# Order of the recurrence and seven waits' places in a three-product float32 decoder kernel, with GpSimd's hold one piece later

## The chip, the cores and the metric

The kernel runs on one core of a Trainium2 chip. Six processors work side by side on it: TensorE (matmuls, results in eight PSUM banks of 128 x 512 float32), VectorE, ScalarE (which loads a table before a new family of functions), GpSimd, SyncE, which issues transfers, and the DMA engines. Each runs its own list of instructions in order and waits for others by semaphores. The metric is the time of one execution in microseconds (us), as a median over runs.

## The reference, cut to what matters

Two blocks over 512 tokens of width 1024, batch 1. The first block has two layers: layer 0 mixes by a bidirectional gated linear recurrence (HGRN2, 8 heads of 128), layer 1 by latent attention (16 heads). Each layer then has an MLP and a gated embedding ("ple"):

```
for i in range(DEPTH):                       # 2 layers
    a = rms_norm(h, pre_mix_norm[i])
    m = hgrn2_mixer(a, ...) if i == 0 else mla_mixer(a, ...)
    h = h + rms_norm(m, post_mix_norm[i])
    f = squared_relu_mlp(rms_norm(h, pre_mlp_norm[i]), w_mlp_in[i], w_mlp_out[i])
    h = h + rms_norm(f, post_mlp_norm[i])
    e = p[i] @ w_ple_proj[i]
    g = sigmoid(h @ w_ple_gate[i])
    h = h + rms_norm(g * e, ple_norm[i])

def step(state, inp):                        # one chunk of the recurrence
    q_dec, k_inv, k_end = qi * exp(G), ki * exp(-G), ki * exp(G_last - G)
    attn = where(mask, q_dec @ k_inv.T, 0)
    o = attn @ vi + q_dec @ state
    new_state = exp(G_last) * state + k_end.T @ vi
```

The recurrence runs forward and backward, and its two outputs are added, normed and multiplied by silu(gate). The second block (names ending in _2) has a differential attention of four heads beside a convolution of 31 taps, a cross attention to a memory of 256 rows (w_ckv_2 gives its keys and values), and a convolutional feed-forward net. Everything is float32.

## The kernel before

**Tiles.** Activations lie feature-major: eight tiles of 128 features x 512 tokens. A float32 matmul is made of three faster ones: each operand x is split into a high half xH, rounded to a shorter type, and a low half xL = x - xH, and TensorE adds H·H, H·L and L·H (`three`, the lines L479 to L481; where three column blocks of weights run side by side, L577 to L582). Weights come from HBM in pieces of 128 rows x 512, in the order of a list PLAN that `plan()` writes. GpSimd splits piece after piece in `split_piece`: a tensor_scalar makes wH (L2775), a tensor_tensor wL (L2777). There are seven split buffers, so piece n waits until TensorE is done with piece n - 7. ScalarE makes the high halves of activations (aH, uH) and VectorE the low halves (aL, uL).

**Hold.** `behind[n] = "x0"` in `plan()` makes GpSimd wait, before it splits piece n, until VectorE has made the last low half of the stream x0 (`add_normed`: the residual plus a normed value, then the norm for the next matmuls). There are six such holds: x (into the MLP), hs (into the gate of the embedding) and n (into the next layer), for each of the two layers. In each, the weights of three column blocks are opened first (`open3`), so that TensorE can take each tile of the stream as it comes.

**Recurrence.** For each head, `recur` in `pe` does for one direction after the other three things: it transposes k_end (L634, "keT"; ScalarE copies the result to g_kT, "kT"), makes the scores (L641, "S"; VectorE masks them), and the states (L650, "U", which read g_kT and the values g_Vt; VectorE accumulates them, "St"). `outputs` (L659) then multiplies the masked scores, summed over both directions in g_As, with the values. Between them stand projections for the next head, and for the last head (7) steps of the out projection. ScalarE in its head loop does the sigmoids of the next head's forget gates and this head's gate ("sg", `sigmoid_g`), then `recur` (the copies kT), then logarithms and decays; for head 7 only the gate's sigmoid, `exp_table()` and `recur`. VectorE does in the same order the gate's product (`out_gate`) and `recur`.

**Norms.** A norm's sum of squares over the features is made by VectorE adding squares of tiles 0 to 6 ("sum") and by two matmuls with ones in `stat_end` (L512 for the sum, L515 for the squares of the last tile, "sq"); ScalarE takes the root as exp(-0.5 ln), for which it needs another table than for the sigmoid. For "ple" ScalarE squares tiles 0 to 6 and VectorE tile 7, after its last sum; ScalarE loads the table for exp and ln meanwhile.

**Around them.** At the start TensorE does the projections of head 0 in the order forward gate, backward gate, statistics "a1", q, out gate, values. In layer 1, between the gate and the next stream, stand the keys of the memory (`memory_keys(0)` ahead of the statistics "ple", `memory_keys(2)` behind). In the differential attention, `d_normed(hd)` on VectorE makes a head's normed output and at once its low half uL, for which it waits for ScalarE's uH; `d_turned(hd + 1)` rescales the next head's attention.

## Time and profile before

| | |
|---|---|
| median of 3 runs | 2334.65 us (2334.12 to 2335.09) |
| profiled execution: its time / its span | 2332.7 us / 2330.9 us |
| TensorE busy | 98% of the span |
| VectorE, ScalarE, GpSimd busy | 55%, 28%, 67% |
| mean granted clock of TensorE | 0.995 |
| chain of work that ended last | TensorE 91%, VectorE 5%, GpSimd 3%, ScalarE 1% |

A row of the trace's order of time begins with the start in us from the start of the span and the duration; then come engine, line, operation, output<-inputs by the program's names, shapes, and the number of instructions that were joined in the row. In brackets stands how long the engine sat idle before it, and what ended the idle time. The granted clock is the share of full speed, 2.4 GHz; 0.5 would be 1.2 GHz.

### The profile page before, as it was taken

What the parts mean: (1) busy time and instruction counts of PE and PEld (TensorE: products, weight loads), DVE (VectorE), ACT (ScalarE), POOL (GpSimd) and SP (SyncE); (2) the same over time, 40 slices, a digit from 0 to 9 for tenths busy, and PEclk for the clock granted to TensorE, in tenths of its full rate; (3) what the DMA queues carried; (4) which work ended last, traced back from release to release, by engine and by line L of the source; (5) the groups of instructions that cost most, each with busy time, mean ns of one, the idle gap of its engine ahead of it and who ended that gap; (6) DMA issues with size and microseconds to landing.
All of it is one profiled execution on the core that took longest, in us unless ns stands there. A gap on an engine that the chain in (4) does not pass through costs nothing.

```text
span 2330.9 us, 27596 instructions
## 1 busy us (share of the span) xinstructions
PE 2280.3 (98%) x10430; PEld 1855.1 (80%) x10430; DVE 1282.2 (55%) x1825; ACT 653.0 (28%) x1202; POOL 1568.7 (67%) x1532
## 2 busy tenths in 40 slices
PE   8999999999999899999999999999999999999998
PEld 6888877888887688888778888787668788888887
DVE  7774737245245777175544364469865445626354
ACT  3443433101013455154311010132344232202113
POOL 8556557877776654644497777678426947878784
PEclk9999999999999999999999999999999999999999
DMA  5222222333332211211243333333212422333332
GB/s 170 77 73 82 72 82 77 109 99 95 100 95 77 72 38 32 81 41 54 69 121 106 96 110 103 95 87 109 64 37 77 122 56 94 99 96 96 99 95 77
DMA packets 112725, 200.16 MB, mean 86 GB/s; under 512 B 12496, under 2 KB 21200, under 8 KB 112592
## 3 DMA queue, kind: packets, MB, share of 16 engines
q1 hardware_dynamic: 109424, 194.72, 29.0%
q10 hardware_dynamic: 3168, 3.67, 0.5%
q8 instruction: 83, 1.36, 0.2%
q14 instruction: 50, 0.41, 0.1%
HBM read 196.24 MB, written 2.10 MB: 85 GB/s over the span
## 4 chain that ended last, share of the span: by engine, by line
PE 91%; DVE 5%; POOL 3%; ACT 1%; issue 0%; DMA 0%; SPq 0%; DVEq 0%; POOLq 0%
PE bank L479 26%; PE bank L481 26%; PE bank L480 26%; POOL wL L2777 2%; PE bank L916 1%; DVE bank L1936 1%; DVE h L1928 1%; POOL wH L2775 1%; PE bank L1040 1%; DVE aL L1936 1%; PE bank L512 1%; PE bank L885 1%; PE bank L887 1%; PE bank L886 1%; PE bank L893 1%; PE bank L894 1%
## 5 line engine op out<-in xcount | busy, mean ns | idle before, releaser
L2777 POOL TENSOR_TENSOR wL<-raw,wH 128x512 fp32r<-128x512 f32 (+2 forms) x732 | 1002.9, 1370 | 61.1
L2775 POOL TENSOR_SCALAR wH<-raw 128x512 fp32r<-128x512 f32 (+2 forms) x732 | 530.0, 724 | 587.3 <-PE bank L481 496.8
L479 PE MATMUL bank<-aH,wH 128*128 128x512 f32 x1376 | 546.5, 397 | 12.7 <-DVE aL L1936 7.0
L481 PE MATMUL bank<-aH,wL 128*128 128x512 f32 x1376 | 536.6, 390 | 0.0
L480 PE MATMUL bank<-aL,wH 128*128 128x512 f32 x1376 | 536.5, 390 | 0.0
L479 PE MATMUL bank<-uH,wH 128*128 128x512 f32 (+1 forms) x978 | 378.4, 387 | 0.0
L481 PE MATMUL bank<-uH,wL 128*128 128x512 f32 (+1 forms) x978 | 376.8, 385 | 0.0
L480 PE MATMUL bank<-uL,wH 128*128 128x512 f32 (+1 forms) x978 | 376.8, 385 | 0.0
L479 PEld LDWEIGHTS bank<-aH,wH 128*128 128x128 f32 x1376 | 258.4, 188 | 73.3 <-POOL wL L2777 13.8
L480 PEld LDWEIGHTS bank<-aL,wH 128*128 128x128 f32 x1376 | 258.6, 188 | 56.5 <-issue 4.1
L481 PEld LDWEIGHTS bank<-aH,wL 128*128 128x128 f32 x1376 | 258.4, 188 | 54.7
L480 PEld LDWEIGHTS bank<-uL,wH 128*128 128x128 f32 x978 | 183.7, 188 | 37.4 <-issue 0.7
L479 PEld LDWEIGHTS bank<-uH,wH 128*128 128x128 f32 x978 | 183.7, 188 | 37.4 <-issue 0.7
L481 PEld LDWEIGHTS bank<-uH,wL 128*128 128x128 f32 x978 | 183.7, 188 | 36.7
L1299 ACT ACTIVATE uH<-mr 128x512 fp32r<-128x512 f32 x64 | 40.5, 633 | 391.0 <-DVE mr L1936 391.0
L1928 DVE TENSOR_TENSOR F<-F,bank 128x512 f32<-128x512 f32 x56 | 38.4, 686 | 190.1 <-PE bank L481 190.1
L1936 DVE SCALAR_TENSOR_TENSOR mr<-bank,rs 128x512 f32<-128x512 f32 x64 | 44.0, 688 | 156.6 <-PE bank L481 140.7
L1936 DVE SCALAR_TENSOR_TENSOR bank<-F,vs,bank 128x512 f32<-128x512 f32 x138 | 103.7, 751 | 35.7 <-ACT bank L1299 22.7
L1928 DVE TENSOR_TENSOR sums<-sums,sq 128x512 f32<-128x512 f32 (+1 forms) x66 | 81.8, 1240 | 69.9 <-ACT sq L1299 69.7
L1928 DVE TENSOR_TENSOR h<-h,bank 128x512 f32<-128x512 f32 (+1 forms) x91 | 60.7, 668 | 97.6 <-PE bank L481 95.9
L2784 POOL TENSOR_SCALAR m_P<-m_P,m_stat 128x512 f32<-128x512 f32 x64 | 44.6, 698 | 92.5 <-DVE m_stat L2370 90.4
L1936 DVE SCALAR_TENSOR_TENSOR c_cb<-c_xb,vs,c_cb 128x511 f32<-128x511 f32 x88 | 82.8, 941 | 40.3 <-ACT c_cb L1299 38.7
(328 smaller groups left out, 3208.9 us busy)
## 6 DMA issues: line engine op xcount, KB each, us to landing
raw<-in_ws SPq DMA_DIRECT2D x698, 256.0 KB, 2.6
raw<-in_ws SPq DMA_DIRECT2D x24, 192.0 KB, 2.3
h<-in_xT SPq DMA_DIRECT2D x8, 256.0 KB, 5.5
E<-in_memT ACTq DMA_DIRECT2D x16, 128.0 KB, 2.7
raw<-in_ws SPq DMA_DIRECT2D x10, 128.0 KB, 2.2
tmp<-in_pT ACTq DMA_DIRECT2D x4, 256.0 KB, 3.2
out<-c_F SPq DMA_DIRECT2D x2, 512.0 KB, 2.9
out<-c_F SPq DMA_DIRECT2D x2, 384.0 KB, 2.9
```

Of the source, the lines that this page charges most:

```text
L479: P.e.matmul(o, lH, rH, start=start, stop=False, skip_group_check=skip)
L480: P.e.matmul(o, lH, rL, start=False, stop=False, skip_group_check=skip)
L481: return P.e.matmul(o, lL, rH, start=False, stop=stop, skip_group_check=skip)
L512: i = P.e.matmul(b.ap[:, 0:n], ones, sums[:, 0:n], start=True, stop=not tail)
L885: P.e.matmul(b.ap[:, :], m_qnH[:, c], m_knH[:, :], start=True, stop=False)
L886: P.e.matmul(b.ap[:, :], m_qnH[:, c], m_knL[:, :], start=False, stop=False)
L1299: return A.e.activation(o, i, func, bias=bias, scale=scale)
L1928: return V.e.tensor_tensor(o, a, b, op)
L1936: return V.e.scalar_tensor_tensor(o, a, s, b, op0, op1)
L2775: G.e.tensor_scalar(H, x, 1.0, 0.0, MUL, ADD).then_inc(*G.did("wH", n))
L2777: G.e.tensor_tensor(L, x, H.bitcast(F32), SUB).then_inc(*G.did("w", n))
L2784: G.e.tensor_scalar(x, x, m_st[:, 4 * (hd % 2) + n, 2:3], 0.0, MUL, ADD).then_inc(*G.did("mP", hd, n))
```

## The change

Seven things are moved, all in the order of work; what is computed stays, only the place where a square is made changes.

1. `plan()`: each hold stands one piece later in the list, so GpSimd splits one piece more before it waits for VectorE (three places in `mlp_ple`, which is called for two layers: six holds).
2. `stat_end` and the embedding: ScalarE squares all eight tiles of "ple", and VectorE's square of tile 7 goes; ScalarE loads its table after the eighth square.
3. `pe`, `recur`: both directions' transposes, then both directions' scores, then both directions' states.
4. Start: the projection of q stands ahead of the statistics "a1".
5. Layer 1: both steps of the memory's keys stand behind the statistics "ple".
6. ScalarE and VectorE, head loop: for heads 0 to 6 the order is as before; for head 7 `recur` stands ahead of the gate's sigmoid, its product and the table load.
7. VectorE, differential attention: the low half of `d_normed` is a function of its own, `d_normed_low`, and stands behind the turning of the next head.

```diff
--- before.py
+++ after.py
@@ -79,21 +79,21 @@
     def mlp_ple(layer, *keys_next):
         embed(layer, 0)
         open3(*[("w_mlp_in", layer, 128 * o) for o in range(3)])
-        behind[len(out)] = f"x{layer}"
+        behind[len(out) + 1] = f"x{layer}"
         for g in range(4):
             for i in range(0 if g else 3, 8):
                 tile8("w_mlp_in", layer, 1024 * g + 128 * i)
             down("w_mlp_out", layer, tuple(range(8 * g, 8 * g + 8)), g == 0)
         embed(layer, 1)
         open3(*[("w_ple_gate", layer, 128 * o) for o in range(3)])
-        behind[len(out)] = f"hs{layer}"
+        behind[len(out) + 1] = f"hs{layer}"
         for o in range(3, 8):
             tile8("w_ple_gate", layer, 128 * o)
         if layer:
             for o in range(4):
                 tile8("w_ckv_2", 0, 128 * o)
         open3(*keys_next)
-        behind[len(out)] = f"n{layer}"
+        behind[len(out) + 1] = f"n{layer}"
 
     mlp_ple(0, *[("mla_w_in", 0, 128 * o) for o in (3, 4, 0)])
     for i in (1, 2):
@@ -511,7 +511,7 @@
                 P.wait_ge(cs_in)
                 i = P.e.matmul(b.ap[:, 0:n], ones, sums[:, 0:n], start=True, stop=not tail)
                 if tail:
-                    P.wait_ge(V if sid[0] == "ple" else A, "sq", sid, tiles - 1)
+                    P.wait_ge(A, "sq", sid, tiles - 1)
                     i = P.e.matmul(b.ap[:, 0:n], ones, sq[:, 0:n], start=False, stop=True)
                 i.then_inc(*P.did("stat", *sid))
                 if adds:
@@ -634,6 +634,7 @@
                         i = P.e.transpose(b.ap[:, cols128(n)], g_ke[d][:, cols128(n)], ident)
                     i.then_inc(*P.did("keT", head, d))
                     give(b, A, "kT", head, d)
+                for d in range(2):
                     b = take("S", head, d)
                     P.wait_ge(V, "ki", head, d)
                     P.wait_ge(V, "qd", head, d)
@@ -642,6 +643,7 @@
                                        start=True, stop=True)
                     i.then_inc(*P.did("S", head, d))
                     give(b, V, "Ab", head, d)
+                for d in range(2):
                     b = take("U", head, d)
                     P.wait_ge(A, "kT", head, d)
                     P.wait_ge(A, "Vt", head // 4, 3)
@@ -676,9 +678,9 @@
 
             project(0, 1)
             project(0, 2)
+            project(0, 0)
             stat_end("a1")
-            for part in (0, 3):
-                project(0, part)
+            project(0, 3)
             project_v(0)
             columns("a1")
             for head in range(8):
@@ -792,12 +794,11 @@
                 for o in range(3, 8):
                     linear(("gate", i, o), (A, "sg", i, o), "w_ple_gate", i, 128 * o, aH, aL, hs_ready)
                 P.also("gate done", i)
-                if i == 1:
-                    memory_keys(0)
                 stat_end("ple", i, adds=f"n{i}")
                 P.also("end ple", i)
                 if i == 1:
-                    memory_keys(2)
+                    for o in (0, 2):
+                        memory_keys(o)
                 P.wait_ge(A, "end ple", i)
                 P.wait_ge(V, "end ple", i)
                 lin = three_open(keys_next, events_next)
@@ -1402,12 +1403,14 @@
                     out_gated(head - 1)
                 if head < 7:
                     sigmoid_f(head + 1, 0)
-                sigmoid_g(head)
                 if head < 7:
+                    sigmoid_g(head)
                     sigmoid_f(head + 1, 1)
+                    recur(head)
                 else:
+                    recur(head)
+                    sigmoid_g(head)
                     exp_table()
-                recur(head)
                 if head < 7:
                     for d in range(2):
                         log_f(head + 1, d)
@@ -1523,11 +1526,9 @@
                     if o > 1:
                         A.wait_ge(V, "Fg", i, o - 2)
                     do(mr[o % 2][:, :], bk("gate", i, o)[:, :], ACT.Sigmoid).then_inc(*A.did("sg", i, o))
-                    if o < 7:
-                        A.wait_ge(V, "Fg", i, o)
-                        square(("ple", i), o, F[:, o, :])
+                    A.wait_ge(V, "Fg", i, o)
+                    square(("ple", i), o, F[:, o, :])
                 exp_table()
-                squares_end[1] = (P, "stat", "ple", i)
                 A.also("end ple", i)
                 A.wait_ge(P, "end ple", i)
                 A.wait_ge(V, "end ple", i)
@@ -2110,11 +2111,14 @@
                 if head < 7:
                     project_f(head + 1, 0)
                     key_gate(head + 1, 0)
-                out_gate(head)
                 if head < 7:
+                    out_gate(head)
                     project_f(head + 1, 1)
                     key_gate(head + 1, 1)
-                recur(head)
+                    recur(head)
+                else:
+                    recur(head)
+                    out_gate(head)
                 if head < 7:
                     for d in range(2):
                         log_decay(head + 1, d)
@@ -2255,9 +2259,6 @@
                     tt(F[:, o, :], E[:, o, :], mr[o % 2][:, :], MUL).then_inc(*V.did("Fg", i, o))
                     if 0 < o < 7:
                         add_squares(("ple", i), o)
-                V.wait_ge(V, "Fg", i, 7)
-                V.wait_ge(V, "sum", ("ple", i), 6)
-                tt(sq[:, :], F[:, 7, :], F[:, 7, :], MUL).then_inc(*V.did("sq", ("ple", i), 7))
                 V.also("end ple", i)
                 V.wait_ge(P, "end ple", i)
                 V.wait_ge(A, "end ple", i)
@@ -2543,9 +2544,11 @@
                 V.wait_ge(A, "rstd", "dn", hd)
                 V.wait_ge(V, *(("rr", 2 * hd + 4) if hd < 2 else ("y2L", hd - 1)))
                 stt(y, bk("do", hd)[:, :], lam[:, 5:6], root("dn", hd), MUL, MUL).then_inc(*V.did("dn", hd))
+
+            def d_normed_low(hd):
                 V.wait_ge(V, "dn", hd)
                 V.wait_ge(A, "y2H", hd)
-                low(uL[:, hd, :], y, uH[:, hd, :]).then_inc(*V.did("y2L", hd))
+                low(uL[:, hd, :], tmp[0][:, :], uH[:, hd, :]).then_inc(*V.did("y2L", hd))
 
             some_taps(27)
             for t in range(4):
@@ -2587,6 +2590,7 @@
                     ts(d_acc[:, BY_PE, :], bk("ctap")[:, :], vv("cv_dw_b_2", BY_PE), None, ADD, None).then_inc(*V.did("conv", BY_PE))
                 d_normed(hd)
                 d_turned(hd + 1)
+                d_normed_low(hd)
             V.wait_ge(P, "mu")
             for i in range(4):
                 V.wait_ge(*((V, "conv", i) if i == BY_PE else (A, "conv", i)))
@@ -2608,6 +2612,7 @@
                 stt(d_acc[:, i, :], d_acc[:, i, :], vv("cv_ln_g_2", i), root("ln"), MUL, MUL).then_inc(*V.did("lnn", i))
             d_turned(3)
             d_normed(2)
+            d_normed_low(2)
 
             def convolved_low(i):
                 V.wait_ge(A, "y2H", 4 + i)
@@ -2616,6 +2621,7 @@
             convolved_low(0)
             convolved_low(1)
             d_normed(3)
+            d_normed_low(3)
             convolved_low(2)
             convolved_low(3)
             xvalues(0)
```

## Rows read from the trace of the kernel before

**Rows 1.** Page: busy us (share of the span) and instructions of each engine.

```profile
PE 2280.3 (98%) x10430; PEld 1855.1 (80%) x10430; DVE 1282.2 (55%) x1825; ACT 653.0 (28%) x1202; POOL 1568.7 (67%) x1532
```

**Rows 2.** TensorE's waits: line, what it waited for: us in total, times, longest.

```profile
PE bank L650 <- ACT g_kT L1299: 8.4, 8, 4.0
...
PE bank L479 <- POOL wL L2777: 4.7, 5, 1.6
```

**Rows 3.** Two stretches, head 1 and 7: length, TensorE busy, clock, DMA share, GB/s.

```profile
99.00:103.61 4.61, 4.01 (x36) 1.00 0.37 114
289.59:299.12 9.53, 5.54 (x36) 0.82 0.11 28
```

**Rows 4.** TensorE in order of time, head 1, second direction.

```profile
101.76 0.49 PE L634 MATMUL bank<-cs,g_ke 128*128 128x128 f32 x3
102.09 1.06 PE L641 MATMUL bank<-g_qd,g_ki 128*128 128x128 f32 x8
102.98 0.85 PE L650 MATMUL bank<-g_Vt,g_kT 128*128 128x128 f32 x6
103.58 0.48 PE L479 MATMUL bank<-aH,wH 128*128 128x512 f32 x1
```

**Rows 5.** Order of time, head 1: ScalarE's copy, VectorE's product, TensorE's outputs.

```profile
100.46 0.47 ACT L1299 ACTIVATE g_kT<-bank 128x384 f32<-128x384 f32 x1
...
104.84 0.69 DVE L1928 TENSOR_TENSOR g_As<-g_Ab 128x512 f32<-128x512 f32 x1
...
109.15 1.05 PE L659 MATMUL bank<-g_As,g_Vt 128*128 128x128 f32 x8
```

**Rows 6.** ScalarE in order of time, head 7.

```profile
291.18 1.28 ACT L1299 ACT_TABLE_LOAD   x1
...
293.12 1.28 ACT L1290 ACT_TABLE_LOAD   x1
294.42 0.49 ACT L1299 ACTIVATE g_kT<-bank 128x384 f32<-128x384 f32 x1
```

**Rows 7.** Order of time, start: the statistics on TensorE, their root on ScalarE.

```profile
22.77 1.13 PE L512 MATMUL bank<-sums,cs 128*128 128x512 f32 x2 [1.25 <-DVE sums L1928]
...
29.09 0.67 ACT L1299 ACTIVATE rs<-bank,cs 128x512 f32<-128x512 f32 x1
```

**Rows 8.** Order of time: VectorE's low half in layer 0 and later, GpSimd's split.

```profile
352.62 0.74 DVE L1936 SCALAR_TENSOR_TENSOR aL<-h,vs,aH 128x512 fp32r<-128x512 f32 x1
...
1804.42 1.29 POOL L2777 TENSOR_TENSOR wL<-raw,wH 128x512 fp32r<-128x512 f32 x1
1804.56 1.70 DVE L1936 SCALAR_TENSOR_TENSOR aL<-h,vs,aH 128x512 fp32r<-128x512 f32 x1 [0.87 <-ACT aH L1299]
```

**Rows 9.** Order of time, layer 0, hold x0: GpSimd resumes, TensorE gets the piece.

```profile
366.63 2.59 POOL L2775 TENSOR_SCALAR wH<-raw 128x512 fp32r<-128x512 f32 x1 [16.02 <-DVE aL L1936]
...
371.47 0.50 PE L479 MATMUL bank<-aH,wH 128*128 128x512 f32 x1 [1.61 <-POOL wL L2777]
```

**Rows 10.** TensorE in order of time, layer 0: statistics "ple", first held piece.

```profile
760.32 1.12 PE L515 MATMUL bank<-sq,cs 128*128 128x512 f32 x2 [2.35 <-DVE sq L1928]
...
784.63 0.50 PE L479 MATMUL bank<-aH,wH 128*128 128x512 f32 x1 [0.91 <-POOL wL L2777]
```

**Rows 11.** Order of time, layer 1: GpSimd resumes; TensorE's start into stream n1.

```profile
1527.22 0.62 POOL L2775 TENSOR_SCALAR wH<-raw 128x512 fp32r<-128x512 f32 x1 [15.50 <-DVE aL L1928]
...
1573.01 0.50 PE L581 MATMUL bank<-aH,wH 128*128 128x512 f32 x1 [1.64 <-POOL wL L2777]
...
1575.39 0.79 PE L581 MATMUL bank<-aH,wH 128*128 128x512 f32 x1 [1.65 <-POOL wL L2777]
...
1578.40 0.40 PE L581 MATMUL bank<-aH,wH 128*128 128x512 f32 x1
```

**Rows 12.** Order of time, differential attention: VectorE's low half, TensorE's next matmul.

```profile
1717.99 0.69 DVE L1928 TENSOR_TENSOR uL<-tmp,uH 128x512 fp32r<-128x512 f32 x1 [1.32 <-ACT uH L1299]
...
1719.89 0.39 PE L1022 MATMUL bank<-d_kH,d_qH 64*128 64x256 f32 x2 [1.99 <-DVE uL L1928]
```

## The prediction, made before the change was run

> **What bounds the kernel now.** I read the busy times first: TensorE is at work for 2280.3 of 2330.9 us, VectorE for 55%, GpSimd for 67% [rows 1]. So some 50 us of TensorE's idle time is all that a reordering can win; no edit here removes a matmul from TensorE. Next, TensorE's waits by line [rows 2] say where part of that lies: at L650 the eight heads of the recurrence wait 8.4 us for ScalarE's copy of the transposed keys, and at L479 TensorE waits five times, 4.7 us, for the low half of a weight piece. The other waits that the change aims at I took from TensorE's own order of time, one by one, with what each row waited for in brackets. The profiled execution took 2332.7 us and lies 1.95 under the median 2334.65; I sum against 2332.7 and add 1.95 at the end.
>
> **Recurrence, heads 0 to 6.** Between the last matmul of the projection before and the first of the one behind lie 4.61 us with 4.01 busy [rows 3]; seven such stretches look alike (4.58 to 4.64). Transposes, scores and states of one direction follow one another, so the states wait for ScalarE's copy of transposes that were made just before. By the starts in [rows 4], one set of transposes takes 102.09 − 101.76 = 0.33, scores 0.89, states 0.60. In the new order both transposes and both scores stand ahead of the first states: 2 × (0.33 + 0.89 + 0.60) = 3.64 if nothing waits, against 4.58: −0.94 for each head, −6.6 for seven. Does the wait come back? The copy is done at 100.46 + 0.47 = 100.93, 1.93 after the start [rows 5]; the states now begin 2 × (0.33 + 0.89) = 2.44 after it, so 0.5 is to spare, and the second copy has as much. VectorE gets the first direction's states 0.45 later and the second's 0.94 earlier. Its last product for the head ends at 104.84 + 0.69 = 105.53, and TensorE's output matmuls, which need it, start at 109.15 [rows 5], 108.2 in the new order: 2.7 to spare.
>
> **Recurrence, head 7.** Its stretch takes 9.53, at a mean granted clock of 0.82 [rows 3]: ScalarE serves the sigmoid of the gate first, between two loads of an activation table (291.18, 293.12), and copies the keys only at 294.42 [rows 6]. The idle time also lets the clock fall from 2.4 to 1.2 GHz for part of the stretch. With the copies ahead of gate and tables the stretch is the 3.64 of the others: −5.9. The gate and its two loads then run after the copies, some 3.9 us on ScalarE (1.30 from load to the next start, twice, with the sigmoid and square between) while TensorE runs the steps of the out projection; the output of head 7 is wanted from ScalarE about 4 us after that, so I charge nothing. If that cover were gone, at most one load, 1.3, would show.
>
> **Start.** TensorE waits 1.25 for VectorE's sum before the statistics of a1 [rows 7]. One projection now stands ahead of it, TensorE starts it 1.25 to 1.4 earlier, and its weights are there: −1.3. The statistics come some 5 us later, but ScalarE takes the root of them only at 29.09 [rows 7], held by another chain (the scalars of the attention); at most 0.3 lies open.
>
> **GpSimd's hold.** Six times GpSimd waits until VectorE has stored the last tile of a normed stream, and only then splits the next piece. One piece more ahead of the hold means that TensorE finds a piece ready 1.96 (one split) earlier, while VectorE may be slowed by it.
>
> First the price. A split's second instruction reads two tiles of SBUF. VectorE's aL alone takes 0.74; begun 0.14 after such a split it took 1.70 [rows 8], 0.96 more. So one extra piece inside VectorE's chain costs between 0 (it falls beside an instruction that takes an operand from PSUM, or in a gap) and 1.9 (both its instructions stop VectorE for their whole length). I take 0.7, near to the 0.96 of the row, less because only one aL of eight can meet it. The Trainium skill speaks against this part of the change: "SBUF — State Buffer", section "Who interferes with whom", says that a VectorE instruction with two SBUF inputs and a GpSimd instruction that reads SBUF exclude each other for a whole instruction, whoever began first. The 1.70 agrees with that for a split that began first; by the page the extra piece would cost up to its whole length at each hold, which is rival A below.
>
> Layer 0 and 1, MLP in: GpSimd resumes at 366.63, with a first half that then took 2.59, and TensorE waits 1.61 for the piece until 371.47 [rows 9]; layer 1 has the same with 1.64. The piece now ready, this wait goes, less 0.7: −0.9 each, −1.8. Late next would be the piece after it, done near 371.8 and wanted near 372.7.
>
> Stream hs, layer 0: it isn't among the five waits at L479, so there is nothing to win and the price stands: +0.7. In layer 1 it is counted with n1.
>
> Stream n0: here the squares of the last tile move from VectorE to ScalarE. VectorE's is the last thing that TensorE waits for, 2.35 until 760.32 [rows 10], being queued behind its sums; ScalarE is free 0.95 earlier. The table load then ends about when the statistics are there, so it takes nothing back: −0.95. The hold's wait of 0.91 at 784.63 [rows 10] goes too; the chain there has some 1.1 of room, so no price: −1.9 together.
>
> Stream n1: from 1527.22 GpSimd splits 24 pieces without a pause and is behind all the time [rows 11]: TensorE waits 1.64 and 1.65 for it at 1573.01 and 1575.39, and the next seven matmuls take 3.01 (to 1578.40) where at 2.4 GHz seven take 1.59, because the clock fell. That is 4.7 in all. One piece ahead is 1.96 of it, less 0.7, and most of the 1.4 of the slow clock goes with the second wait: between −0.7 and −3.3, I take −2.8, since only one wait of the two can remain. The keys of the memory that are moved behind the statistics let VectorE's chain start 3.3 earlier, but GpSimd bounds here: nothing for themselves.
>
> **Lows of the differential attention.** At 1717.99 VectorE has waited 1.32 for ScalarE's high half, and TensorE starts 1.99 late at 1719.89 [rows 12]. With the turning of the next head put in between, VectorE does what TensorE waits for first: −1.8. The other two heads are covered by the convolution's mean.
>
> **Sum.** −6.6 − 5.9 − 1.3 − 1.8 + 0.7 − 1.9 − 2.8 − 1.8 = −21.4: 2332.7 − 21.4 = 2311.3, and as a median 2313.2. With every bound at its best (heads −7.0, head 7 −6.4, the holds with no price −3.25, 0, −1.9, −3.3, start −1.35, lows −2.0: −25.2) it is 2309.4 as a median; I go to 2308.5 for the spread of runs. With the small ones at their worst (head 7 1.3 less, n1 −0.7, lows −0.8) it is 2317.6.
>
> **Rivals.** A, the hold's extra piece stops VectorE for all of its 1.9: then four holds that lie in a chain (both MLP streams, hs0, and n1 with hs1) cost 1.2 more each, and n0's room of 1.1 is exceeded by 0.8: 5.6, and 0.7 for hs1: 6.3 less, 2319.5. For it is the 1.70 of [rows 8]; against it is that most of VectorE's instructions there leave gaps while they wait for ScalarE. Chance 0.10.
>
> B, the recurrence of heads 0 to 6 gives nothing: the 0.94 comes back as a wait at the output matmuls (L659) or as a later copy. Gain 14.8: 2319.9. Against it are the 0.5 and 2.7 to spare. Chance 0.08.
>
> C, slower: VectorE's chain from states to the product that L659 waits for becomes the last thing in every head, because its first direction starts later. Eight heads pay, 8 us for each us of wait; the kernel becomes slower by over 4.7 if the wait exceeds (21.4 + 4.7)/8 = 3.3, that is if the product slips by more than 2.7 + 3.3 = 6.0. A wait of 3.5 gives −21.4 + 28 = +6.6: 2341.2. Against it: the first direction's states come only 0.45 later. Chance 0.03.
>
> D, the loads of the activation table cost more than the profile's 1.30 from start to start [rows 6], and so the new square ahead of the load at n0 and n1 starts the norm late. The Trainium skill, "ScalarE: Activation LUTs", section "What ACT_TABLE_LOAD costs", gives about 1.28 for the load and about 1.38 for a drain ahead of it, 2.66 a switch. The two rows here don't show the drain as time between them. With 1.36 more at n0, its 0.95 turns into +0.4 and n1 hides it: gain 20.0, 2314.6. Chance 0.04.
>
> E, no difference: the waits removed at TensorE reappear at the next barrier (each stage ends in one that VectorE and ScalarE must reach), so less than 4.7 is left: about 2333. Against it: GpSimd is 67% busy and VectorE 55%, and in the recurrence TensorE is 87% busy inside the stretch, with projections on both sides that wait for nobody. Chance 0.05.
>
> **How the numbers follow.** The forecast holds 0.70; A and B 0.18, D 0.04, E 0.05, C 0.03. Predicted is the forecast's 2313.2. The range must take in A and B (2319.9): 2308.5 to 2321. E and C, and tails, are left out: about 0.1 to 0.15. About 0.2% of the time, 4.7 us, is what a measurement of this kernel can tell from no change: faster by more 0.92 (forecast, A, B, D), within it 0.05 (E), slower 0.03 (C).
>
> **What would show it.** Right: no row at L650 with a wait, stretches of 3.64 for all eight heads with a clock of 1.00; no wait for the low half at the opening of both MLPs; the wait at the statistics of layer 0's gate near 1.4 instead of 2.35; one wait instead of two near 1573 less 20; none at L1022. Wrong: L659 with waits (B, C); aL or h on VectorE lengthened to 1.7 or more at the holds, and the opening later than before by over 1 (A); a copy of keys that starts late because ScalarE is still on the gate's sigmoid. The weakest terms are n1 and the price of the hold.

## The result and the profile after

The changed kernel takes 2309.9 us as a median of four runs (2309.46 to 2310.26), beside 2334.39 of the kernel before on the same chip: a ratio of 0.9896, with a 95% interval from 0.9879 to 0.9914. That is 24.5 us less; forecast were 21.4 less, 2313.2, in a range from 2308.5 to 2321. The profiled execution took 2309.96 with a span of 2308.2, which is 22.7 shorter than the span of before. TensorE is busy for 99% of it.

Six of the lines on TensorE's waits of the kernel after (line, what it waited for: us in total, times, longest; the changed kernel's line numbers are up to 6 higher than those of before):

```profile
PE bank L581 <- DVE bank L1937: 5.5, 3, 3.9
PE bank L515 <- ACT sq L1300: 3.3, 3, 1.4
PE bank L581 <- POOL wH L2781: 1.8, 2, 0.9
PE bank L577 <- DVE aL L1937: 1.6, 4, 0.6
PE bank L1023 <- DVE uL L1929: 0.6, 1, 0.6
PE bank L479 <- POOL wL L2783: 0.6, 2, 0.3
```

The line for the copy of the keys is gone, and the waits at L479 for a weight's low half fell from 4.7 to 0.6 [rows 2]. Two kinds of wait are longer than before: the one for the last square at L515 (three times instead of one for ScalarE's) and short ones for aL at L577.

The recurrence of the kernel after, heads 0 and 7 (length, TensorE busy, granted clock, DMA share, GB/s):

```profile
68.60:72.33 3.73, 3.73 (x36) 1.00 0.33 81
282.51:286.24 3.73, 3.73 (x36) 1.00 0.20 70
```

Both stretches are full, where head 1 had 4.61 with 4.01 busy and head 7 had 9.53 at a clock of 0.82 [rows 3]. All eight run 3.69 to 3.70 from the first transpose to the next projection.

Where the time went is read best by setting the start of one and the same matmul in both traces side by side, behind each stage:

| behind | before | after | after − before | the stage alone | forecast |
|---|---|---|---|---|---|
| start (first transposes of head 0) | 69.34 | 68.60 | −0.74 | −0.74 | −1.3 |
| heads 0 to 6 | 273.39 | 266.34 | −7.05 | −6.31 | −6.6 |
| head 7 | 299.09 | 286.21 | −12.88 | −5.83 | −5.9 |
| stream x0 | 373.42 | 359.15 | −14.27 | −1.39 | −0.9 |
| stream hs0 | 728.60 | 714.89 | −13.71 | +0.56 | +0.7 |
| stream n0 | 785.89 | 771.05 | −14.84 | −1.13 | −1.9 |
| stream x1 | 1173.83 | 1157.57 | −16.26 | −1.42 | −0.9 |
| streams hs1 and n1 | 1582.98 | 1563.97 | −19.01 | −2.75 (+0.56 and −3.31) | −2.8 |
| lows of the attention | 1726.99 | 1704.29 | −22.70 | −3.69 | −1.8 |

Nothing changes behind that. The sum, −22.7, is 1.3 beyond the forecast's −21.4, and made of terms that miss in both directions.

### The profile page after: what moved, and what is told of

Same layout as the page of the kernel before. It is cut to its first block, busy times and chain, and to the rows that moved or that the text cites. A ratio compares the mean times of both kernels' runs of the same rounds, so it can differ in the third digit from the quotient of the medians.

```text
span 2308.2 us, 27603 instructions
## 1 busy us (share of the span) xinstructions
PE 2274.4 (99%) x10430; PEld 1852.0 (80%) x10430; DVE 1284.8 (56%) x1823; ACT 653.0 (28%) x1204; POOL 1575.7 (68%) x1532
## 3 DMA queue, kind: packets, MB, share of 16 engines
q8 instruction: 83, 1.36, 0.2%
## 4 chain that ended last, share of the span: by engine, by line
PE 93%; DVE 3%; POOL 2%; ACT 1%; DMA 0%; issue 0%; SPq 0%; DVEq 0%; POOLq 0%
PE bank L479 27%; PE bank L481 27%; PE bank L480 27%; POOL wL L2783 1%; PE bank L917 1%; PE bank L1041 1%; DVE bank L1937 1%; DVE h L1929 1%; PE bank L577 1%; PE bank L512 1%; PE bank L581 1%; POOL wH L2781 1%; PE bank L582 1%; DVE aL L1937 1%; PE bank L886 1%; PE bank L887 1%
## 5 line engine op out<-in xcount | busy, mean ns | idle before, releaser
L479 PE MATMUL bank<-aH,wH 128*128 128x512 f32 x1376 | 546.2, 397 | 8.9 <-DVE aL L1937 7.5
L479 PE MATMUL bank<-uH,wH 128*128 128x512 f32 (+1 forms) x978 | 378.5, 387 | 0.0
L479 PEld LDWEIGHTS bank<-aH,wH 128*128 128x128 f32 x1376 | 258.4, 188 | 68.4 <-POOL wL L2783 6.5
L479 PEld LDWEIGHTS bank<-uH,wH 128*128 128x128 f32 x978 | 183.7, 188 | 37.4 <-issue 0.7
```

Source lines behind the costliest of these rows:

```text
L479: P.e.matmul(o, lH, rH, start=start, stop=False, skip_group_check=skip)
```

## The experiments

All of them ran against the kernel before on the same chip. Differences against the changed kernel are taken from medians where both ran on one chip (the first four runs), otherwise from the ratios; what belongs to one stage is read by the same marks as in the table.

**The changed kernel again.**

> The changed kernel again, as the base on this chip for the runs beside it: 2309.9 us against 2334.4 of the kernel before, a difference of 24.5; its profiled span was 22.7 shorter than the one of before, so the true difference lies between 22.5 and 25.

2308.8 against 2332.7, ratio 0.9896 (0.9883 to 0.9910): 23.9 less, inside what was expected. Its trace differs from that of the first run in two places: 0.79 less at the start, and 0.98 less at stream n0. At the start it isn't the clock: the matmuls run at the higher level from 12.84 on in the first trace and only from 13.24 on in the second. It is VectorE's last low half for the first projection. In the first trace it begins 0.38 after a wL of GpSimd (13.59), takes 1.77, and TensorE waits for it:

```profile
13.97 1.77 DVE L1937 SCALAR_TENSOR_TENSOR aL<-h,vs,aH 128x512 fp32r<-128x512 f32 x1
15.89 0.47 PE L479 MATMUL bank<-aH,wH 128*128 128x512 f32 x1 [0.76 <-DVE aL L1937]
```

In the second it begins 0.64 ahead of GpSimd's wL (13.41 and 14.05) and takes 1.10, and TensorE doesn't wait. At n0 it is the clock. The stream n0 opens behind a wait of 3.92 in both, at the lower of the two levels. TensorE's order of time there, first the kernel after, then the same kernel again, with the stretch up to the same matmul (length, busy, clock, DMA share, GB/s):

```profile
750.68 0.77 PE L581 MATMUL bank<-aH,wH 128*128 128x512 f32 x1 [3.92 <-DVE bank L1937]
...
756.37 0.53 PE L581 MATMUL bank<-aH,wH 128*128 128x512 f32 x1
...
750.68:757.66 6.98, 6.98 (x19) 0.57 0.13 38
```

```profile
749.89 0.76 PE L581 MATMUL bank<-aH,wH 128*128 128x512 f32 x1 [3.92 <-DVE bank L1937]
...
753.85 0.39 PE L581 MATMUL bank<-aH,wH 128*128 128x512 f32 x1
...
749.89:755.92 6.03, 6.03 (x18) 0.67 0.15 43
```

The same work took 6.98 and 6.03, because the clock rose 5.7 and 4.0 after the opening. In six more runs below this stage ended between 0.09 and 1.25 earlier than in the first profile, with nothing changed in it.

**GpSimd's holds back at their old place.**

```diff
-        behind[len(out) + 1] = f"x{layer}"     # the same for hs and n
+        behind[len(out)] = f"x{layer}"
```

> The changed kernel with GpSimd's six holds back at their old place. Theory (each post-norm with an extra piece pays for one lengthened aL, 0.35 to 0.45, since VectorE's aL took 1.27 beside the split instead of 0.74 in the profile after; the waits that the hold cost come back): x0 and x1 +1.25 each, hs0 and hs1 -0.4 each, n0 +0.9, n1 +2 to +3 because GpSimd is again one piece (1.96) later there; sum +4.6 to +5.6 over the changed kernel. aL at the x0 opening takes 0.74 again. Rival (the extra piece stops VectorE for its full 1.9 at each hold): the waits that come back are nearly paid by the price that goes, sum under +1.

2314.28: +5.5 over the changed kernel on this chip. The sum is as the theory had it, two of its terms aren't: by the marks n1 costs 4.0, and at n0 a wait of only 0.25 comes back. The rival's under +1 is out. The price of the hold is seen directly. Stream x0, GpSimd's extra piece beside VectorE's first aL and what TensorE waits for, kernel after:

```profile
339.18 1.29 POOL L2783 TENSOR_TENSOR wL<-raw,wH 128x512 fp32r<-128x512 f32 x1
339.75 1.27 DVE L1937 SCALAR_TENSOR_TENSOR aL<-h,vs,aH 128x512 fp32r<-128x512 f32 x1
341.07 0.96 PE L577 MATMUL bank<-aL,wH 128*128 128x512 f32 x3 [0.23 <-DVE aL L1937]
```

and with the holds at their old place:

```profile
339.09 0.74 DVE L1937 SCALAR_TENSOR_TENSOR aL<-h,vs,aH 128x512 fp32r<-128x512 f32 x1
...
357.94 0.50 PE L479 MATMUL bank<-aH,wH 128*128 128x512 f32 x1 [1.60 <-POOL wL L2783]
```

One aL of eight takes 1.27 instead of 0.74, which makes TensorE 0.5 late by the marks; against that stands the wait of 1.60 that is back. Only in n1 the undone hold costs much more than the piece is long: +4.0, with two waits, and a granted clock that is down behind the second:

```profile
1559.09 0.50 PE L581 MATMUL bank<-aH,wH 128*128 128x512 f32 x1 [0.77 <-POOL wL L2783]
1561.47 0.50 PE L581 MATMUL bank<-aH,wH 128*128 128x512 f32 x1 [1.65 <-POOL wL L2783]
```

**The old order of the recurrence on TensorE.**

```diff
-                for d in range(2):        # before the scores, and before the states
```

> The changed kernel with the old order of transposes, scores and states on TensorE; everything else as changed. Theory: the wait of 0.6 to 0.7 for the copy of the keys is back in each of eight heads, and with the idle time of filling and draining the stretch is 4.58 to 4.64 instead of 3.70: +7.2 (8 times 0.9); no wait at the outputs in either. Rival (the recurrence's order gives little, because the wait moves to the output matmuls or to the projections behind): under +2, with the stretches at 4.6 and a wait less elsewhere.

2315.86: +7.1, as the theory had it. TensorE's waits show eight of them again, 0.60 to 0.69 each, and the stretches are 4.57 to 4.64:

```profile
PE bank L650 <- ACT g_kT L1298: 5.0, 8, 0.7
```

**Head 7's gate and tables ahead of the copies again.**

```diff
+                sigmoid_g(head)
                 if head < 7:
-                    sigmoid_g(head)
                     sigmoid_f(head + 1, 1)
-                    recur(head)
                 else:
-                    recur(head)
-                    sigmoid_g(head)
                     exp_table()
+                recur(head)
```

(VectorE's `out_gate` likewise.)

> The changed kernel with the gate's sigmoid, its product and the table load of head 7 ahead of the key copies on ScalarE and VectorE, as before; TensorE keeps the new order. Theory: the copies start some 4.8 us after the stretch begins (the two table loads and the sigmoid first), TensorE is at the states after 2.44 and so waits about 2.9; the granted clock may fall behind the wait as it did before (0.82 in that stretch), which adds up to 1.7: +2.9 to +4.6. Rival (TensorE's new order already covers the copies, the move on ScalarE gives nothing): 0.

2312.56: +3.8; the stretch is 8.02 long with a wait of 2.87. ScalarE and TensorE in order of time, and the stretch (length, busy, clock, DMA share, GB/s):

```profile
283.12 1.28 ACT L1300 ACT_TABLE_LOAD   x1
284.42 0.63 ACT L1300 ACTIVATE tmp<-g_sg 128x512 f32<-128x512 f32 x1
285.07 1.28 ACT L1291 ACT_TABLE_LOAD   x1
286.36 0.87 ACT L1300 ACTIVATE g_kT<-bank 128x384 f32<-128x384 f32 x2
...
287.00 2.90 PE L652 MATMUL bank<-g_Vt,g_kT 128*128 128x128 f32 x12 [2.87 <-ACT g_kT L1300]
...
281.53:289.55 8.02, 5.15 (x36) 0.81 0.10 33
```

So head 7's −5.8 needs both edits. TensorE's order alone gives 1.5 of it and leaves 4.3 (8.02 against 3.73); the place of the gate alone gives 4.9, since in the run above, with TensorE's old order, head 7 takes only 0.9 more than in the changed kernel.

**Memory's keys: first half ahead of the statistics again.**

```diff
+                if i == 1:
+                    memory_keys(0)
                 stat_end("ple", i, adds=f"n{i}")
                 P.also("end ple", i)
                 if i == 1:
-                    for o in (0, 2):
-                        memory_keys(o)
+                    memory_keys(2)
```

> The changed kernel with the first half of the memory's keys again ahead of the statistics of layer 1's gate. Theory: TensorE's wait of 1.38 there, which the profile after shows at 1544.17, is covered again, but VectorE's chain for the stream n1 starts about 4.2 later; it has 5.3 in hand at the first tile and loses 0.36 on each of seven further tiles, so the last tile comes about 1.4 late: -1.4 + 1.4 = 0, within 1. Rival 1 (GpSimd alone sets the pace at n1, as the prediction said): -1.4 to 0, with waits for wL and none for aL. Rival 2 (the head start of VectorE is worth its whole length): +3.

Ratio 0.9910 (0.9894 to 0.9927) against the changed kernel's 0.9896: +3.3 with intervals that overlap, and +3.8 in stream n1 by the marks. The theory (0, within 1) fell, and so did the first rival; the size is that of the second, the mechanism isn't quite. TensorE waits first for GpSimd and then, at the closing statistics of the stream, for VectorE's sums of the residual:

```profile
1556.23 0.50 PE L581 MATMUL bank<-aH,wH 128*128 128x512 f32 x1 [1.10 <-POOL wL L2784]
1574.77 2.07 PE L526 MATMUL bank<-F,cs 128*128 128x512 f32 x2 [2.19 <-DVE F L1930]
...
1577.07 0.63 PE L480 MATMUL bank<-aL,wH 128*128 128x512 f32 x1
```

After the second wait the matmuls run at the lower clock again: 0.63 each against 0.39. In the kernel after, the same statistics start without a wait, 0.26 after VectorE's last sum has ended (1571.34 + 1.67 = 1573.01):

```profile
1573.27 1.02 PE L526 MATMUL bank<-F,cs 128*128 128x512 f32 x2
```

**Lows straight behind the norm again.**

```diff
-                d_turned(hd + 1)
                 d_normed_low(hd)
+                d_turned(hd + 1)
```

> The changed kernel with the low half of the differential attention's norm again straight behind the norm. Theory (the removed wait also kept the clock up: before, the eight convolution matmuls behind the wait took 5.34, after it 3.65): the wait of 1.99 is back, +2.0, and the granted clock falls behind it, +1.7: +3.7. Rival (the fall of the clock there had nothing to do with this wait): +2.0, with the eight matmuls at 3.65.

Ratio 0.9915 (0.9900 to 0.9929), which is +4.4 by the ratios, with intervals that overlap; by the marks the stage costs 3.7, as the theory had it. TensorE's order of time there, and below it the row of the kernel after that answers to the second:

```profile
1700.11 0.39 PE L1023 MATMUL bank<-d_kH,d_qH 64*128 64x256 f32 x2 [1.99 <-DVE uL L1929]
...
1700.93 5.34 PE L1041 MATMUL bank<-F 128*128 128x512 f32 x8
```

```profile
1699.72 3.65 PE L1041 MATMUL bank<-F 128*128 128x512 f32 x8
```

The eight matmuls behind the wait take 5.34 instead of 3.65: 1.69 of the stage is the clock, 1.99 the wait.

**Last square on VectorE again.**

```diff
-                    P.wait_ge(A, "sq", sid, tiles - 1)
+                    P.wait_ge(V if sid[0] == "ple" else A, "sq", sid, tiles - 1)
...
+                tt(sq[:, :], F[:, 7, :], F[:, 7, :], MUL).then_inc(*V.did("sq", ("ple", i), 7))
```

(ScalarE squares tiles 0 to 6.)

> The changed kernel with the last square of each gate again on VectorE. Theory: TensorE waits for the statistics 2.35 instead of 1.38, at both layers (layer 1 no longer has the memory's keys ahead of them): +0.95 at n0, and at n1 0 to +0.95, depending on whether VectorE's chain or TensorE is late there; the time for which the clock is low at n0 can move by up to 0.9 either way. Sum +0.5 to +2. Rival (the table load takes back what ScalarE's square gains): 0.

Ratio 0.9907 (0.9892 to 0.9922): +2.6 by the ratios, above the expected range, but not resolved by the times. By the marks +1.06 at n0 and +2.0 at n1, where TensorE waits 2.38, as at n0, and the clock falls at 1545:

```profile
1545.35 1.22 PE L515 MATMUL bank<-sq,cs 128*128 128x512 f32 x1 [2.38 <-DVE sq L1931]
```

**Statistics a1 at their old place.**

```diff
-            project(0, 0)
             stat_end("a1")
+            project(0, 0)
             project(0, 3)
```

> The changed kernel with the statistics a1 again ahead of the projection of q. Theory: TensorE waits 1.25 for VectorE's sum again; in the profile after, 1.17 was won there, of which 0.4 was lost because the clock rose 0.9 later than before, which this edit doesn't touch: +1.2. Rival (the later statistics delay the first head, so that the move is worth only 0.7 or less): +0.3 to +0.7.

Ratio 0.9902 (0.9888 to 0.9917): +1.4 by the ratios, which the times can't resolve. The wait of 1.25 is back in the trace. From the last matmul ahead of the moved projection to the first transposes of head 0, this trace takes 1.5 more than the one of the changed kernel, and so does the kernel before; that is the theory, and the rival is out. The transposes themselves lie only 0.26 later, because the matmuls ahead of the move, which the edit doesn't touch, were 1.2 earlier in this execution, mostly because it lacks the wait of 0.76 for VectorE's last low half. In nine more traces with the new start the first transposes lay 0.29 later to 0.99 earlier than in the profile after.

**One part alone in the kernel before: the holds.**

```diff
-        behind[len(out)] = f"x{layer}"     # the same for hs and n
+        behind[len(out) + 1] = f"x{layer}"
```

> The kernel before with GpSimd's six holds one piece later and nothing else of the change. Theory of the prediction (GpSimd alone bounds n1): x0, x1, hs0 and n0 as priced, and n1 -2.8: -4.8 in all. Theory from the profiles since (at n1 TensorE needs three chains at once: GpSimd's pieces, VectorE's low halves and VectorE's closing sums, and a head start of one alone only moves the wait to the next): x0 and x1 -1.25 each, hs0 and hs1 +0.4 each, n0 -0.9, n1 0 within 1, with a wait of about 2 for VectorE's sums at its end: -2 to -3.5 in all.

Ratio 0.9988 (0.9979 to 0.9997): −2.8, between −4.9 and −0.7. The prediction's −4.8 lies at the edge of that, so the time alone doesn't decide; the marks do. x0 and x1 give 1.4 each, n1 loses 0.9 instead of winning 2.8. (All the holds' terms together are −0.9 in this profile, which is the slowest of the eleven executions, 1.8 above their median; so nothing is concluded from its small terms; the 3.7 between forecast and measured at n1 are far above that.) There TensorE waits once for GpSimd, and then for VectorE's sums, with the clock down behind it:

```profile
1573.23 0.50 PE L581 MATMUL bank<-aH,wH 128*128 128x512 f32 x1 [1.51 <-POOL wL L2777]
...
1591.75 1.22 PE L526 MATMUL bank<-F,cs 128*128 128x512 f32 x1 [2.17 <-DVE F L1928]
```

**One part alone in the kernel before: the keys.**

```diff
-                if i == 1:
-                    memory_keys(0)
                 stat_end("ple", i, adds=f"n{i}")
                 P.also("end ple", i)
                 if i == 1:
-                    memory_keys(2)
+                    for o in (0, 2):
+                        memory_keys(o)
```

> The kernel before with both steps of the memory's keys behind the statistics of layer 1's gate and nothing else of the change. Theory of the prediction: GpSimd bounds there, so 0. Theory from the profiles since: TensorE's wait for VectorE's last square, 2.35 as at layer 0, is no longer covered, the clock can fall behind it (1.4), GpSimd's pieces come no earlier and the stream takes that time up again only in part: 0 to +2, never faster. Rival (the earlier start of VectorE's chain is worth most of its 3.3 by itself): -1.5 to -3.

Ratio 1.0003 (0.9995 to 1.0012): no difference that could be measured. By the marks the stage is 1.06 shorter, so "never faster" was wrong for the stage, and the rival's 1.5 to 3 was too much. The wait for VectorE's square is uncovered, as expected:

```profile
1563.70 0.70 PE L515 MATMUL bank<-sq,cs 128*128 128x512 f32 x1 [2.30 <-DVE sq L1927]
```

**Filling the wait at the statistics.** The changed kernel with hs0's hold at its old place and four of the eight steps of the first keys, 12 matmuls, ahead of the statistics:

```diff
-        behind[len(out) + 1] = f"hs{layer}"
+        behind[len(out) + layer] = f"hs{layer}"
...
+                if i == 1:
+                    begun = take("xk", 0), block("w_ckv_2", 0, K8, ((0, 128),))
+                    fm(begun[0], begun[1], 0, 128, x_mH, x_mL, m_ready, n=256, at=0, ks=range(4))
                 stat_end("ple", i, adds=f"n{i}")
```

> The changed kernel with two edits: the hold of hs0 back at its old place (hs1 stays later), and the first quarter of the memory's first keys, 12 matmuls or 1.4 us, ahead of the statistics, into TensorE's wait of 1.38 there. Theory: the wait is filled and the statistics are not later, but VectorE's closing sums of n1 end at 1573.0 in the profile after and TensorE needs them at 1573.3, so only 0.3 of the 1.4 is kept and the rest becomes a wait at the next statistics; hs0 gives 0.4: -0.4 to -0.7 against the changed kernel, which the times can't resolve but the order of time can. Rival (TensorE's own work is what is late at n1): -1.8.

Ratio 0.9888 (0.9874 to 0.9901), 2308.2: below the changed kernel's 0.9896, but the intervals overlap, so it isn't shown to be faster. By the marks hs0 gives the 0.6 that its lengthened aL had cost, and n1 gives nothing (+0.05). The wait at the statistics of layer 1 is gone, and its 1.38 is added almost whole to the first wait for GpSimd, 0.30 before:

```profile
1556.25 0.50 PE L583 MATMUL bank<-aH,wH 128*128 128x512 f32 x1 [1.65 <-POOL wL L2793]
```

The theory had the direction; it named VectorE's sums as next late, and GpSimd's piece came first.

**Each hold one piece later still.**

```diff
-        behind[len(out) + 1] = f"x{layer}"     # the same for hs and n
+        behind[len(out) + 2] = f"x{layer}"
```

> The changed kernel with each hold one piece later still, so two pieces are split beside VectorE's chain. Theory (the price is a split's second instruction meeting an aL, and no wait is left at the openings to pay for it): x0, x1, hs0 and hs1 0 to +0.5 each, n0 0, n1 -0.3: 0 to +1.5, with a second lengthened aL of 1.0 to 1.3 in each chain. Rival (a head start of GpSimd is worth its length wherever it is behind): -1 to -2.

Ratio 0.9897 (0.9882 to 0.9913): no difference from one piece, within the expected 0 to +1.5; the rival is not seen. By the marks x0 and x1 give 0, hs0 and hs1 cost 0.1 each, and n1 costs 0.3 where it was to give 0.3: the wait of 0.30 for GpSimd is gone, and one of 0.62 for VectorE's closing sums has come. The second lengthened aL did not come. The second extra piece waits for TensorE to give a buffer free (GpSimd is idle for 7.46 until 347.31), and its wL begins after an aL, not ahead of it:

```profile
347.85 0.74 DVE L1937 SCALAR_TENSOR_TENSOR aL<-h,vs,aH 128x512 fp32r<-128x512 f32 x1
348.01 1.74 POOL L2783 TENSOR_TENSOR wL<-raw,wH 128x512 fp32r<-128x512 f32 x1
```

This time aL takes its usual 0.74 and GpSimd's wL 1.74 instead of 1.29.

## Why the prediction was right, and where its steps were not

**Recurrence.** Right in size and reason. A stretch is 3.70, where the starts of one direction gave 3.64. VectorE's product ends at 103.89 and TensorE wants it at 106.57, so there are still 2.7 to spare; rivals B and C had no ground. For head 7 the copies run at 284.00 and the two tables behind them, ahead of the output of the head at 292.84; the cover of the tables held.

**Start.** Right: the wait of 1.25 went, and from the last matmul ahead of the move on the kernel is 1.5 faster, against 1.3. Only 0.74 arrived in the profile, because the matmuls ahead, which the change doesn't touch, were 0.76 later there. That is the wait of 0.76 at 15.89 shown with the first run, and not the clock, as the expectation of the run on a1 had it: in the second trace of the changed kernel the clock rises later still, the wait is missing, and these matmuls end as early as before. The order of the statistics cost nothing.

**Holds, x and hs.** The mechanism was right, the price too high: 0.5 to 0.6 measured for each, 0.7 taken, and rival A's 1.9 is excluded by the undone holds. The prediction had put against each other an aL that met a split (1.70) and one alone [rows 8]; what decides is which of the two begins first. With wL first, aL waited for it (1.27); with aL first, wL waited (1.74). The Trainium skill says so ("SBUF — State Buffer", section "Who interferes with whom": the exclusion lasts a whole instruction and goes by who was first). These two rows agree on who waits; the delays, 0.53 and 0.45, are somewhat less than what was left of the other instruction (0.72 and 0.58). At x0 the gain ahead of the price was mis-sized too: 1.9 by the marks and not 1.6, since the matmuls behind the wait started slowly as well.

**Stream n0.** Forecast −1.9, −1.13 in the profile and −2.11 in the second trace of the same kernel. Wait for the square (2.35 to 1.38) and wait for the piece (0.91 to none) went as worked out. TensorE's statistics, ScalarE's load and its root in the kernel after:

```profile
745.63 1.13 PE L515 MATMUL bank<-sq,cs 128*128 128x512 f32 x2 [1.38 <-ACT sq L1300]
745.60 1.28 ACT L1291 ACT_TABLE_LOAD   x1
746.89 0.66 ACT L1300 ACTIVATE bank<-bank,cs 128x512 f32<-128x512 f32 x1
```

The table load ends at 746.88 and the root starts at 746.89, when the statistics (745.63 + 1.13) have just ended, so rival D's extra 1.36 doesn't exist here. The drain of about 1.38 that the Trainium skill counts with a load ("ScalarE: Activation LUTs", section "What ACT_TABLE_LOAD costs") isn't seen on either side of it, neither here nor in the undone gate, where the load at 285.07 begins 0.02 after the activation ahead of it has ended (284.42 + 0.63) and the copy 0.01 after the load. What the sum didn't have is that the clock's rise falls at another place of the work each time, and that the wait for the held piece had been hiding this. From the opening of n0 to the mark, the three traces with this hold at its old place (before, the keys alone, the undone holds) take 20.65, 20.67 and 20.69, although the first part, 6.98 and 6.03 in the two traces of the changed kernel, takes 6.08, 6.20 and 6.76 in them: the piece sets the time, and TensorE waits for it 0.91, 0.80 and 0.25. With the hold later TensorE waits for no piece, and the whole takes 19.1 to 20.4 in eleven traces, by the clock. So the hold is worth about 0.3 to 1.5 here, by the execution.

**Stream n1.** The number was right by luck and the step behind it wrong. The prediction said that GpSimd bounds there, that the hold gives 2.8 (the terms that it lists, 1.96 − 0.7 + 1.4, come to at most 2.66) and the move of the keys nothing, though it had seen that VectorE starts 3.3 earlier by it. The runs say: the hold alone makes the stage 0.9 longer, the keys alone make it 1.1 shorter, both with the square 3.3 shorter. Undone one at a time, hold, keys and square cost 4.0, 3.8 and 2.0, together 9.8 for a stage that won 3.3. In the changed kernel two chains end within 0.3 us of TensorE there (GpSimd's pieces 0.30 behind it, VectorE's closing sums 0.26 ahead):

```profile
1557.72 0.50 PE L581 MATMUL bank<-aH,wH 128*128 128x512 f32 x1 [0.30 <-POOL wL L2783]
1571.34 1.67 DVE L1929 TENSOR_TENSOR F<-F 128x512 f32<-128x512 f32 x1
```

So a head start of one is worth nothing while another is behind, and taking one away costs its length and, where the wait grows long, the clock. VectorE's closing sums weren't in the prediction at all: "GpSimd bounds here" was read from the two waits that it had caused [rows 11], without asking for the chain just behind it. The fill run shows the same once more: 1.38 of TensorE's idle time closed, 1.35 opened at the next wait.

**Lows.** Right in the reason, half in size: −3.7 instead of −1.8. The term left out is the clock. The prediction counted it for head 7 and for n1, but here stopped at the wait [rows 12], though the row of the eight convolution matmuls behind it already stood in the trace of before:

```profile
1720.72 5.34 PE L1040 MATMUL bank<-F 128*128 128x512 f32 x8
```

The undone lows brought both parts back, 1.99 and 1.69. Against the sign "none at L1022", a second wait of 0.6 in this line stays as it was.

**What a reordering can win.** The prediction put it at TensorE's idle time, some 50 us. Of the 22.7 by which the span shrank, 5.9 are busy time: the same 10430 matmuls took 2274.4 instead of 2280.3, at a mean granted clock of 0.997 instead of 0.995.

**From the sum to the median.** 1.3 of the 3.3 by which 2313.2 was too high are these terms. The other 2.0 come from adding 1.95 for the distance between the profiled execution of before and its median. The changed kernel's profiled execution lies at its median, so nothing was to be added. In the run of the changed kernel again, nine executions of the kernel before have a median of 2332.7, the very time of the profiled one, so the distance isn't a fixed one. A likely reason, which was not tried by itself, is that the kernel before has four places where the clock falls, besides its last microseconds, and the changed one a single place. Head 7 of before takes 9.53 in the profile [rows 3], but with the very same wait of 3.99 it took 10.34 in the kernel that has only the holds moved:

```profile
290.42:300.76 10.34, 6.35 (x36) 0.70 0.08 25
```

If that is the reason, a profile in which the clock was lucky at such places is shorter than the median, and a change that removes the places gains more than the two profiles show.

## What to carry to other kernels

Where a stage waits for one engine, look up when the other chains into it end before counting a head start: it is worth at most the distance to the next one, and undoing parts one by one will then add up to several times what they won together. A wait of TensorE of some 2 us should be priced with the matmuls behind it, read at the level of the clock at which they ran: in this kernel it nearly doubled the term of the lows (1.99 and 1.69). Where a wait ends with another engine's work, it swallows what the clock costs ahead of it, and with the wait gone that cost shows (n0). An extra instruction on GpSimd beside a chain of VectorE costs by who begins first, so place it by its start, not by its length.

## What the runs showed of the hardware that was not expected

The clock did not fall after waits of 1.61 at x0, 1.38 at layer 1's statistics and 1.65 at n1 in the fill run; it fell with those of 1.99 (lows), 2.17 and 2.19 (closing sums), 2.30 and 2.38 (square) and 2.87 (head 7), and with the second of two that came close together (0.77 and 1.65; 1.64 and 1.65). How much it then costs is not set by the wait: the stretch with the same wait of 3.99 took 10.34 and 9.53, and the opening of n0 at the lower level lasted 4.0 and 5.7 us with identical work. The Trainium skill ("TensorE: Matmul & The Clock Gate", section "Part 1: The HAM clock gate") says that the chip's watch on TensorE's activity is free-running and doesn't start anew with a kernel, so that the place of a change differs from run to run; these rows agree. One profile therefore knows such a term only to about 1 us, and a comparison of two profiles of this kernel is not sure below that.
